# Third norm of a two-layer block done one token tile at a time, with the first two query blocks and first scores of tile 0 ahead of those of tile 1

## The reference, cut to what matters

```python
h2 = rmsnorm_2(x, norm2_g) * (1 + scale2) + shift2      # "third norm" of the kernel
# peer(h2): q = h2 @ w_query (16 blocks of 128 columns: 8 heads, two halves each)
#   scores of each half against 128 keys; top 16 of each; top 16 of the 256 sums
#   out = sum_j softmax(score)_j * gelu(h2 . expert_u[e_j]) * expert_v[e_j]
x = x + gate2 * peer(h2, w_query, sub_keys_1, sub_keys_2, expert_u, expert_v)
return rmsnorm_2(x, final_g)
```

## Time and profile before

| | |
|---|---|
| median of 3 runs | 2408.84 us (2408.3 to 2409.6) |
| the profiled execution | 2411.41 us, span in the profile 2409.7 us |
| granted clock of PE, mean | 0.959 of full |
| busy share PE, DVE, ACT, POOL | 87%, 69%, 36%, 26% |
| moved by DMA | 754.31 MB, mean 313 GB/s over the span |
| POOL's fetches of expert rows | 512, from 922.7 us to 2382.7 us |

### The profile page before, as it was taken

How to read it: one execution, slowest core, us unless ns; L and a number is a source line. 1 busy time by engine, 2 the same in 40 slices (tenths; PEclk the granted TensorE clock), 3 DMA queues, 4 the chain that set the end, 5 groups by cost and what they waited for, 6 DMA issues and landing times.

```text
span 2409.7 us, 26622 instructions
## 1 busy us (share of the span) xinstructions
PE 2091.9 (87%) x8894; PEld 1495.3 (62%) x8894; DVE 1666.0 (69%) x3729; ACT 872.0 (36%) x2126; POOL 633.8 (26%) x606
## 2 busy tenths in 40 slices
PE   7999998899999998998996897688788977777776
PEld 3444787788888887877775787577644432323322
DVE  5563645466647737999998898876666666676654
ACT  2321335521103213323325565367643333332322
POOL 2100000000110002333344334344434443434342
PEclk9999998999999999999998998798889999999999
DMA  8631120266684447999999999999999999999997
GB/s 350 198 120 52 36 65 7 96 219 234 247 302 140 137 152 313 406 417 403 415 417 420 419 417 417 375 402 419 420 421 421 421 421 421 414 422 421 421 421 298
DMA packets 131790, 754.31 MB, mean 313 GB/s; under 512 B 14544, under 2 KB 14672, under 8 KB 65616
## 3 DMA queue, kind: packets, MB, share of 16 engines
q0 software_dynamic: 87456, 588.90, 60.0%
q1 hardware_dynamic: 44208, 163.84, 18.6%
HBM read 750.59 MB, written 2.10 MB: 312 GB/s over the span
## 4 chain that ended last, share of the span: by engine, by line
PE 43%; DMA 30%; DVE 17%; ACT 6%; issue 4%; another core or an unknown queue 0%; POOL 0%; DVEq 0%; SPq 0%; ACTq 0%; POOLq 0%
PE PS L605 41%; DMA arena<-experts_dram,ecur 25%; DVE arena L2652 5%; DVE arena L1921 4%; DMA ring<-down_dram 2%; DVE h_all L1921 2%; PE PS L1160 1%; DVE ring L1921 1%; DVE arena L1915 1%; DMA ring<-up_dram 1%; ACT L1786 1%; ACT arena L1790 1%; ACT arena L1796 1%; DMA ring<-branch_dram 1%; ACT const L1798 1%
## 5 line engine op out<-in xcount | busy, mean ns | idle before, releaser
L605 PE MATMUL PS<-h_all,ring 128*128 128x256 f32 (+2 forms) x3584 | 897.3, 408 | 21.1 <-DVE ring L1921 7.5
L2844 POOL DMA_INDIRECT arena<-experts_dram,ecur x512 | 584.5, 1142 | 1089.5 <-PE PS L1160 379.6
L2652 DVE CUSTOM_DVE_ANT_0 arena<-arena 128x1024 f32<-128x1024 f32 x512 | 625.9, 1222 | 293.3 <-DMA arena<-experts_dram,ecur 288.4
L605 PEld LDWEIGHTS PS<-h_all,ring 128*128 128x128 f32 x3584 | 681.7, 193 | 211.5 <-issue 104.7
L605 PE MATMUL PS<-arena,const 128*128 128x512 f32 (+1 forms) x1056 | 496.3, 618 | 134.9 <-ACT const L1798 126.4
L605 PEld LDWEIGHTS PS<-arena,const 128*128 128x128 f32 x1056 | 198.4, 196 | 417.3 <-issue 217.6
L1160 PE MATMUL PS<-const,arena 128*128 128x128 f32 x1304 | 193.0, 305 | 106.3 <-ACT arena L1796 103.2
L1786 ACT ACTIVATE arena<-arena 128x2 f32<-128x2 f32 x255 | 51.6, 202 | 644.0 <-DVE arena L2652 641.3
L605 PE MATMUL PS<-arena,ring 128*128 128x256 f32 x1088 | 245.4, 384 | 11.9 <-DMA ring<-down_dram 7.5
L1160 PEld LDWEIGHTS PS<-const,arena 128*128 128x128 f32 x1304 | 170.0, 158 | 130.0 <-ACT arena L1796 112.1
L605 PEld LDWEIGHTS PS<-arena,ring 128*128 128x128 f32 x1088 | 205.9, 192 | 46.1 <-DMA ring<-down_dram 13.1
(11 more groups left out here) (281 smaller groups left out, 1683.2 us busy)
## 6 DMA issues: line engine op xcount, KB each, us to landing
ring<-up_dram SPq DMA_DIRECT2D x88, 512.0 KB, 3.4
ring<-w_in_dram SPq DMA_DIRECT2D x80, 512.0 KB, 3.9
arena<-ada_dram POOLq DMA_DIRECT2D x80, 512.0 KB, 5.3
ring<-w_out_dram SPq DMA_DIRECT2D x32, 512.0 KB, 5.1
ring<-query_dram SPq DMA_DIRECT2D x32, 512.0 KB
ring<-down_dram SPq DMA_DIRECT2D x16, 704.0 KB, 5.8
ring<-branch_dram SPq DMA_DIRECT2D x16, 512.0 KB
arena<-experts_dram,ecur POOLq DMA_INDIRECT x512
```

The lines of the kernel that those rows point to most:

```text
L605: return nc.tensor.matmul(o, l, r, start=start, stop=stop)
L2652: V.tensor_tensor_reduce(out=u, in0=u, in1=hrow[:, (r // HEADS) % 2, :], scale=1.0, scalar=0.0, op0=MUL, op1=ADD, accum_out=dots[:, p % NB ...
L2844: nc.gpsimd.indirect_dma_start(out=ring_e[:, g % RING, :], out_offset=None, in_=a["experts"], in_offset=bass.IndirectOffsetOnAxis(ap=ecur[ ...
```

## The change

The third norm of half 0 is split into its two token tiles of 128: square root, reciprocal, products, scale and shift each run as 128x128 instead of 128x256. The first two query blocks are done for tile 0 (`query_tile(m, 0)`), then their key scores (`key_scores_tile(0)`), then the same for tile 1. In the order of the engines:

- the weight list becomes up 0, query 0, query 1, up 1, query 2 to 7, up 2;
- PE does both tiles of query blocks 0 and 1 and their scores ahead of `expand(1)`, and the turns of tile 0's rows after it;
- ACT puts `apply_tile(0)` ahead of `up_tap(0)`, cuts `apply_tile(1)` into three parts around the takings-out of tile 0, and copies the turned rows of tile 0 itself (`keep_rows(0, ...)`), which DVE did;
- DVE does `norm_tile(0)`, `norm_tile(1)`, `expanded(0)`, `route(0)`, `expanded(1)`, `route(1)`; `route(0)` waits for the scores of tile 0 alone;
- the counts of the semaphores are moved to fit.

```diff
-    order += [("w_out_2", 0, m) for m in range(KT)] + [("up", 1, 0), ("up", 1, 1)]
-    order += [("query", 0, m) for m in range(EARLY)] + [("up", 1, 2)]
+    order += [("w_out_2", 0, m) for m in range(KT)] + [("up", 1, 0), ("query", 0, 0), ("query", 0, 1), ("up", 1, 1)]
+    order += [("query", 0, m) for m in range(2, EARLY)] + [("up", 1, 2)]
...
+            def query_tile(m, c):
+
+                w = weights("query", 0, m)
+                t = slice(c * P, (c + 1) * P)
+                for k in range(KT):
+                    if m == 0:
+                        pe.wait_ge(h3_ready, KT * c + k + 1)
+                    ins = mm(PS[:, bank("query", 0, m), t], w[k], hv[:, 0, k, t], k == 0, k == KT - 1)
+                ins.then_inc(half_done if c else first_queries, 1)
+
+            def key_scores_tile(c):
+
+                t = slice(c * P, (c + 1) * P)
+                if c:
+                    pe.wait_ge(sc2_ready, c)
+                for m in range(2):
+                    pe.wait_ge(q_ready, 2 * c + m + 1)
+                    ins = mm(PS[:, 6, m * P:(m + 1) * P], qT[:, m, t], mat("keys2") if m else mat("keys1"))
+                ins.then_inc(sc2_done, 1)
...
             expand(0, KT // 2, KT)
+            for c in range(2):
+                query_tile(0, c)
+                query_tile(1, c)
+                key_scores_tile(c)
             expand(1)
-            query(0, 0)
-            query(0, 1)
-            key_scores(0, 0)
             turn_rows(0, 0, 0)
             turn_rows(0, 1, 1)
-            key_scores(0, 1)
             turn_rows(1, 0, 7)
...
+            def root_tile(c):
+
+                t = slice(c * P, (c + 1) * P)
+                act.wait_ge(sq3_used, SUMS3[1])
+                A(rs3[:, t], PS[:, 5, t], ACT.Sqrt, bias=eps, scale=1.0 / D).then_inc(std3_ready, 1)
+
+            def apply_tile(c, lo, hi):
+
+                t = slice(c * P, (c + 1) * P)
+                act.wait_ge(mod_ready, 4)
+                for k in range(lo, hi):
+                    act.wait_ge(normed3, KT * c + k + 1)
+                    h = hv[:, 0, k, t]
+                    A(h, h, ACT.Identity, bias=mod[:, 1, 24 + k:25 + k], scale=eff[:, 3, k:k + 1]).then_inc(h3_ready, 1)
...
+            def keep_query_tile(m, c):
+
+                t = slice(c * P, (c + 1) * P)
+                act.wait_ge(half_done if c else first_queries, TURN["query", 0, m] + 1 if c else m + 1)
+                A(qT[:, m, t], PS[:, bank("query", 0, m), t], ACT.Copy).then_inc(q_ready, 1)
+
+            def keep_scores_tile(c):
+
+                act.wait_ge(sc2_done, c + 1)
+                A(sS[:, 0, c, 0, :, :], PS[:, 6, :HF].rearrange("p (z n) -> p z n", n=NKEYS), ACT.Copy).then_inc(sc2_ready, 1)
...
-            root3(0)
+            root_tile(0)
+            root_tile(1)
+            apply_tile(0, 0, KT)
             up_tap(0)
-            apply3(0)
+            apply_tile(1, 0, 2)
+            keep_query_tile(0, 0)
+            apply_tile(1, 2, 5)
+            keep_query_tile(1, 0)
+            keep_scores_tile(0)
+            apply_tile(1, 5, KT)
+            keep_query_tile(0, 1)
+            keep_query_tile(1, 1)
+            keep_scores_tile(1)
             up_tap(1)
-            keep_query(0, 0)
-            keep_query(0, 1)
-            keep_scores(0, 0)
-            keep_scores(0, 1)
+            keep_rows(0, 0, 0)
+            keep_rows(0, 1, 1)
             keep_rows(1, 0, 7)
...
+            def norm_tile(c):
+
+                t = slice(c * P, (c + 1) * P)
+                dve.wait_ge(std3_ready, c + 1)
+                V.reciprocal(rs3[:, t], rs3[:, t]).then_inc(vec_step, 1)
+                dve.wait_ge(vec_step, n(vec_step))
+                dve.wait_ge(x3_ready, KT)
+                for k in range(KT):
+                    tt(hv[:, 0, k, t], xT[:, k, t], rs3[:, t], MUL).then_inc(normed3, 1)
...
-            norm3(0)
+            norm_tile(0)
+            norm_tile(1)
             expanded(0)
-            expanded(1)
...
-            for t in range(2):
-                dve.wait_ge(hr_done, t + 1)
-                copy(hrow[:, 0, t * S:(t + 1) * S], PS[:, t, :]).then_inc(hr_ready, 1)
             for r in range(2):
                 for j in range(TOPK):
                     route(r, j)
+                if r == 0:
+                    expanded(1)
             gate_sum(0)
             gate_scale(0)
             expanded(2)
```

More of the change, by code:

```diff
@@ L465, in build @@
         q_ready = sem("q_ready")
+        first_queries = sem("first_queries")
         qkv_ready = sem("qkv_ready")
@@ L534, in evicted, with query_kept @@
                 return x2_ready, KT + m + 1
-            return q_ready, 16 * half + m + 1
+            return query_kept(half, m)
+        def query_kept(half, m):
+            return q_ready, 16 * half + m + 3
         def score_banks(n):
@@ L1127, in square_sum @@
                     if s == 1:
-                        pe.wait_ge(std3_ready, 1)
+                        pe.wait_ge(std3_ready, 2)
                 mm(PS[:, 5, :HF], ones, sq4[:, k % 4, :], k == 0, k == KT - 1).then_inc(sq3_used, 1)
@@ L1312, in beside @@
                 if 0 < c < NC - 1 and q == 48:
-                    pe.wait_ge(h3_ready, 3 * KT)
+                    pe.wait_ge(h3_ready, 4 * KT)
                     pe.wait_ge(xrow_ready, 2 * c)
@@ L1721, in keep_rows @@
                 act.wait_ge(hr_done, 2 * c + half + 1)
-                act.wait_ge(hr_ready, 2 * c + half)
+                if c + half:
+                    act.wait_ge(hr_ready, 2 * c + half)
                 if c > 1:
```

17 lines of the change are left out of this document (7 added, 10 removed).

## The result

The changed kernel took 2414.64 us (median of 22 runs, 2410.53 to 2420.86), the kernel before, on the same chips, 2410.22 us (22 runs, 2408.28 to 2413.63). The ratio is 1.002, with a 95% interval of 1.0014 to 1.0025: 4.8 us more, with 3.4 to 6.0 as its bounds. The kernel became slower, by about the 0.2% that the prediction took for the least that can be told; the interval leaves no change out. The plain medians differ by 4.4 us. The forecast was 2412.0, which is 3.2 us above the median it started from. Its direction was right and its amount 1.6 us short: 2414.64 lies above its own range (2410.7 to 2413.4) and inside the wide one (2405 to 2416.5). It had given 0.31 to a kernel that is slower by more than 0.2%, and 0.55 to one that is within it.

The account below looks back on a forecast made before the run. PE's work before expand(2) was taken to bound the first dot: 3.7 us later, less 0.7 won back, gives 3.0; on the median 2408.84, plus 0.2 unplaced, 2412.0 us. Own range 2410.7 to 2413.4, wide 2405 to 2416.5.

Parts of the forecast that it names:

- What bounds it: Start of expert loop: PE's work between sum of squares and expand(2) bounds the first dot at 942.50, not the fetches.
- The route starts earlier: Tile stage: route(0) starts at 908.0 instead of 913.34, 5.3 us earlier, with POOL's first fetch near 917.4.
- PE's list: PE up to query(0, 2): waits and smaller tiles cost 3.7 us, start at 917.3; expand(2) and first dot equally late.
- Weight loads: SP's query and up loads: query 0 and 1 land by 902, up 1 not needed before 912; nothing is paid.
- the rival of the late loads: Query 5 to 7 and up 2 loads fall into full transfers, costing 1.6 to 2.2 us; about 2415, chance 0.20.
- The way to the end: First dot to end: 3.7 us less 0.7 won back gives 3.0; a 5 us hole eats the fetches' lead.
- The load under full transfers: DMA queues shared packet by packet: load time doesn't depend on fetch queue length, so no 0.7 won back; sum 3.7.
- The fetches set the end: Rival: transfers never run dry after 920, so the end follows the first fetch, 5.3 us earlier, 2403.5; chance 0.13.
- The two cancel: Rival: the fetches' lead shortens weight loads on the chain, winning back 2 to 4 us; time 2409; chance 0.20.
- The clock falls: Rival: PE's idle of some 4 us from 900.5 drops its clock, query tiles cost double; 2415.5; chance 0.07.

Follow-up runs that it names:

- the two runs with idle products: Kernel before with 16 or 10 idle 128x256 products on PE ahead of query(0, 2): 2417.52 against 2409.98 us, and 2418.65 against 2410.03 us.
- the held fetch in the changed kernel: Changed kernel, with POOL holding its first fetch until query block 2 is done: 2414.79 us against 2409.98 us for the kernel before.
- Giving back the cover: Changed kernel with expand(1) back ahead of the query tiles, so PE has work while tile 0 is scaled: 2412.13 us, 1.0004 of the kernel before.
- the dot is early: Changed kernel with expanded(2) and up_tap(2) behind the first pairs' work: 2406.32 against 2410.21 us; with the first fetch also held: 2409.74 against 2410.03 us.
- 7.7 us at the dot alone: Kernel before with expanded(2) and up_tap(2) moved behind the first pairs' own work, first fetch as before: 2410.79 against 2410.21 us.
- both together: Changed kernel with expanded(2) and up_tap(2) moved behind the first pairs' own work: 2406.32 us against 2410.21 us for the kernel before.
- the last two runs: Changed kernel with expanded(2) moved behind the first pairs' work, plus expand(1) back ahead of the query tiles (2407.24 us) or the first fetch held (2409.74 us).
- the fetch of the kernel before is held: Kernel before, with POOL holding its first fetch until query block 5 is done: 2413.61 us against 2409.98 us for the kernel before.

## Why the prediction was right or wrong

**What bounds it.** Right in the main. That the first dot is bound by PE's list and not by the fetches is shown by the two runs with idle products (fetch unmoved, dot 7.8 and 6.6 us later, 8 us more) and by the held fetch in the changed kernel (4.4 us later, the same dot and time). One small thing it passed over: PE's list before has a gap of 0.32 us ahead of the last scores, for ACT, which had late word of query block 6.

**The route starts earlier.** Right. `route(0)` starts at 908.70 and the first fetch is at 918.10, with 908.0 and 917.4 forecast; against t0 the gain is 5.6 us, forecast 5.3. The reciprocal of 128 columns took 0.95, as the two rows of before had given it.

**PE's list.** Right. `query(0, 2)` is 3.55 us late, forecast 3.7, and starts at 918.02 instead of 917.3 in a profile whose t0 is 0.94 later. Giving back the cover took 2.0 of the 3.55.

**Weight loads: this step failed.** The prediction put this term at nothing. It said that nothing is paid, and that the six blocks behind `query(0, 2)` and `expand(2)` come late by 3.7 too. They came 5.4 late: PE waited 1.68 and 0.33 us for weights. The working stood in the rival of the late loads, with 8.9 us per load against the 7.8 that PE gives, and 1.6 to 2.2 us as its price; the loads took 9.40 and 8.50 us, and PE waited 2.0 us for them. It fell on two blocks and not on four at 0.4 each, since each stall gives the two loads under way its own length; over the four blocks the rival's sum, an even pace of 4.3 us, comes to nearly the same. The row that was held against the rival, that PE had not waited for up 2 in the full time, was one load, issued at 928.43 and wanted 8.6 us later, as PE had been held up by 0.32 us. The forecast's sum with this term, 3.0 + 1.86, is 4.9, and 4.8 was measured. The rival named the early fetches as the reason. For query block 5 of the changed kernel that is so: with the fetch held its wait is gone. But PE's blocks coming later put loads into the full time as well (0.92 and 1.16 us with the idle products). The waits ahead of up 2 in the held fetch, with ten idle products and with the cover back (1.67, 1.36 and 1.14 us) are no measure of it: there the loads took 8.0 to 8.2 us and were issued 1.7 to 2.8 us late.

**The way to the end.** The amount came out near: 5.4 us at the dot became 4.8, 0.6 won back where 0.7 was forecast. That is luck, with an interval of 3.4 to 6.0 and with 6.6 us at the dot that became 8.0 in another run; and the reason given for it was wrong. The hole is there, between 950 and 960, 7.2 us of transfers where 5 were forecast, and the tenth fetch is at 957.10 after 28.03 us (954.5 and 26 forecast, the difference again the loads). But the claim that all is levelled near 974 does not hold. There the transfers are full (422 GB/s), and the surplus is not gone: DVE, which in the kernel before had a wait at 972.23 and three for rows from 1011 on, waits for its first row at 1050.05, for 0.22 us:

```profile
1050.05 1.23 DVE L2719 CUSTOM_DVE_ANT_0 arena<-arena 128x1024 f32<-128x1024 f32 x1 [0.22 <-DMA arena<-experts_dram,ecur]
```

What the end follows over all eleven kernels is how many bytes the start has moved, which counts the lead of the fetches as well as the hole. That the bytes are the cause, and not something that goes with them, is the account's reading; no run changed them alone. The forecast reasoned from DVE.

**The load under full transfers.** The Trainium skill says in DMA: Bandwidth & Descriptors, section Queues, rings and completion order, that each DMA engine goes round the queues it has work for and changes from one to the next packet by packet. The trace agrees in the main: the load of query block 5 was issued with three of the nine fetches given out, and from 925.3 the weights have a third of the engines' time beside them. The rule does not tell of the 3.6 us before that. What the prediction drew from it, that a load's time does not depend on how many fetches stand queued, is borne out as far as two loads go: in the kernel before, one issued at 935.71, with all nine given out, has 0.01 MB moved by 938.5, and from then to 942 the weights have a third as well. The loads on the chain took 9.40, 8.50, 7.97 and 9.49 us here, 9.44 and 8.36 before. The sum that it gave, 3.7, was nearer to what was measured than 3.0, which rested on shorter loads. It is not the reason for the rest: that is the loads' waits.

**The rivals.** *Loads late* is what happened. Its 2415 is near the 2414.64 measured in part by luck: it was counted from 2408.84, 5.3 to 6.8 us more, and the kernel before took 2410.22 this time, so that 4.8 was measured. *The fetches set the end* fell as it was put, since the transfers did run dry, but something of it holds once the dot is early: there 4.5 us at the fetch are worth 3.3 at the end. Its condition, that the ring must reach to the first dot, which nine slots don't, was the right one to ask for. *The two cancel* fell: the loads on the chain became no shorter. *The clock falls* did not come: 1.00 in the window from 903, although PE works there at the pace of ACT. PE was busy for 3.23 of the 4.00 us from 899 and for all four from 903, more than the working had given it. What the Trainium skill says in TensorE: Matmul & The Clock Gate, section on psum-queue depth-cycling, that frequent short idles between groups of products can throw the clock back and forth, did not happen in these windows.

**What stays open.** Ten idle products cost as much as 16: 6.6 against 7.8 us at the first dot, 8.0 against 7.7 at the end. Of the 6.6 us the doses explain 4.3, and 1.16 and 1.36 are waits for loads. The intervals of the two times overlap almost wholly, so the runs don't tell whether there is more to explain. What holds back the word of a finished block is open too. In nine of the ten traces that have it, this word comes 12.8 to 13.1 us behind the first fetch, wherever that stands, in the tenth after 10.0; so it goes with the nine fetches, but no run took it apart. And no run has the earlier fetch with the first dot where it was before, or takes the late loads away and leaves the rest.

## What to carry to other kernels

Where a ring of slots feeds a loop, two moments set how it starts: when the first slot is filled and when the first one is freed. Here bringing one forward alone won nothing (4.4 us at the fetch with the late dot: 0.3 us, within the noise; 7.7 us at the dot alone: nothing), and both together won 3.1. The change lost because it paid for the earlier fetch with a later dot. Before an order is turned round to start something early, read from PE's timeline which block filled its wait for the other engines, and what is queued behind it; and when the load of a block falls into the full transfers, give it the time of such a load from the trace (8 to 9.5 us here) and not that of a quiet one.

Count the bytes moved up to a fixed moment: of two orders of the same work in front of a stretch bound by transfers, the one that had moved more ended first in these eleven kernels, wherever the times can be told apart. And before a wait is put down to a long load, look at when the load was issued and when the block that it waits for ended.

## What was not expected of the hardware

The weight loads take 8 to 9.5 us in the full time, and up to 3.6 us of it pass before anything is moved for them. One that is too long stalls PE at one block in three, so the place where PE stalls moves with small shifts: 1.68 us at query block 5 in the changed kernel, 0.92 there with 16 idle products, 1.16 at query block 6 with ten.

The word that a block is done can reach ACT and SP 1.3 to 3.4 us behind the end that PE's rows show, while PE goes on with the next block: in ten of eleven traces, and both engines go on at the same moment. In the profile it is a wait for "remote" or "another core or an unknown queue", in a kernel of one core. It stands ahead of the waits for up 2 in the changed kernel with the fetch held, with ten idle products, with the cover back, and in the last two runs (1.67, 1.36, 1.14, 1.15 and 1.48 us), and of the 1.4 us at the first dot where the fetch of the kernel before is held.

And the bytes moved in 200 of 2400 us, read from one execution, told the timed difference of nine of the ten kernels within its interval.
